# One VectorE running sum in place of seven TensorE sums in three norms, and three late modulation sums moved

## What is computed

```python
mod = silu(c) @ w_mod + b_mod                      # 9 vectors of 1024
sh1, sc1, ga1, sh2, sc2, ga2, sh3, sc3, ga3 = split(mod, 9)
h = modulate(rms_norm(x, g_ffn1), sh1, sc1)
x = x + 0.5 * (1 + ga1) * swiglu(h, w1_gate, w1_up, w1_down)     # first FFN, hidden width 2816
h = modulate(rms_norm(x, g_mix), sh2, sc2)
x = x + (1 + ga2) * hybrid_mixer(h, w_in, ...)                   # 16 attention heads, w_o
h = modulate(rms_norm(x, g_ffn2), sh3, sc3)
x = x + 0.5 * (1 + ga3) * swiglu(h, w2_gate, w2_up, w2_down)     # second FFN
```

## Time and profile before

| | us |
|---|---|
| median of 3 runs | 2854.35 (2852.21 to 2855.42) |
| the profiled execution | 2856.67 |
| its span, first to last instruction | 2854.9 |
| PE busy | 2518.7 (88%) |
| DVE busy | 1047.9 (37%) |
| ACT busy | 465.7 (16%) |
| mean granted TensorE clock | 0.939 of full speed |

### The profile page before, as it was taken

One profiled execution on the slowest core, in us unless ns is written; L12 is line 12 of the kernel. 1 busy time (PEld: TensorE's weight loads), 2 busy tenths in 40 slices (PEclk: granted clock), 3 DMA queues, 4 the chain that ended last, 5 costly groups with the idle time before them and its releaser, 6 DMA issues. The chain is left out here.

```text
span 2854.9 us, 24606 instructions
## 1 busy us (share of the span) xinstructions
PE 2518.7 (88%) x9051; PEld 1170.1 (41%) x9051; DVE 1047.9 (37%) x1236; ACT 465.7 (16%) x732; POOL 179.6 (6%) x458
## 2 busy tenths in 40 slices
PE   8999999999998999999997798688888788878884
PEld 4444444465564444434444454333333233323331
DVE  3655530145462333310106633433333333333334
ACT  2000000155332000000102130011111111111111
POOL 0000000000000000000000000111111111111110
PEclk9999999999899999999998799799899989999997
DMA  7444534122101121413201000799999999999995
GB/s 269 147 147 147 175 129 105 33 51 61 49 1 59 59 88 59 120 41 90 86 19 64 0 8 30 310 413 417 411 412 407 411 406 404 410 405 413 403 413 222
DMA packets 182831, 563.19 MB, mean 197 GB/s; under 512 B 16864, under 2 KB 132848, under 8 KB 156544
## 3 DMA queue, kind: packets, MB, share of 16 engines
q1 hardware_dynamic: 172384, 554.10, 50.8%
q0 software_dynamic: 10400, 8.42, 1.0%
HBM read 567.19 MB, written 20.97 MB: 206 GB/s over the span
## 5 line engine op out<-in xcount | busy, mean ns | idle before, releaser
L1143 PE MATMUL ps<-slot,xT 128*64 128x512 f32 x2048 | 516.4, 663 | 164.6 <-DMA slot<-in_expert_w_up 163.9
L715 PE MATMUL ps<-hT,slot 128*128 128x512 f32 x1408 | 614.4, 597 | 13.0 <-ACT hT L1238 7.2
L715 PEld LDWEIGHTS ps<-hT,slot 128*128 128x128 f32 x1408 | 267.9, 192 | 351.0 <-issue 347.4
L1143 PEld LDWEIGHTS ps<-slot,xT 128*64 128x64 f32 x2048 | 155.6, 152 | 523.5 <-issue 304.5
L743 PE MATMUL ps<-big,slot 128*128 128x512 f32 x704 | 310.4, 601 | 12.0 <-DVE big L1565 6.2
L1974 DVE COPY hT<-ps 128x256 f32<-128x256 f32 x64 | 27.2, 425 | 632.0 <-PE ps L1151 632.0
L1162 PE MATMUL ps<-slot,hT 128*64 128x512 f32 x1024 | 235.6, 602 | 1.2 <-DVE hT L1974 1.2
L1965 DVE RECIPROCAL xT<-xT 64x512 f32<-64x512 f32 x64 | 214.1, 3345 | 2.2
L743 PEld LDWEIGHTS ps<-big,slot 128*128 128x128 f32 x704 | 135.7, 193 | 182.0 <-issue 169.0
L1561 DVE RECIPROCAL eb<-eb 128x512 f32<-128x512 f32 x44 | 147.5, 3353 | 1.5
L1559 DVE TENSOR_SCALAR eb<-eb 128x512 f32<-128x512 f32 x44 | 18.8, 427 | 331.8 <-ACT eb L1248 331.8
(11 more groups left out here) (331 smaller groups left out, 2313.2 us busy)
## 6 DMA issues: line engine op xcount, KB each, us to landing
slot<-in_expert_w_gate SPq DMA_DIRECT2D x64, 2048.0 KB, 19.4
slot<-in_expert_w_up SPq DMA_DIRECT2D x64, 2048.0 KB, 22.7
slot<-in_expert_w_down SPq DMA_DIRECT2D x64, 2048.0 KB, 25.0
slot<-in_w_mod SPq DMA_DIRECT2D x18, 2048.0 KB, 8.0
slot<-in_w_gate SPq DMA_DIRECT2D x22, 1024.0 KB, 5.5
slot<-in_w_up SPq DMA_DIRECT2D x22, 1024.0 KB, 7.9
slot<-in_w_down SPq DMA_DIRECT2D x16, 1408.0 KB, 7.4
slot<-in_w_in SPq DMA_DIRECT2D x24, 512.0 KB, 6.4
```

What stands on the lines that cost most here:

```text
L715: last = mm(ps[:, 2 * j + g, :], w[:, g, k, j * P:(j + 1) * P], hT[:, k, META:TOK], start=(k == 0), stop=(k == KC - 1))
L1143: last = mm(ps[g * CAP:(g + 1) * CAP, j, :], xsT[j][:, k, :], w[g][:, k, :], start=(k == 0), stop=(k == KC - 1))
```

## The change

In norms 1, 2 and 3 TensorE's eight sums become two. ScalarE writes the square of chunk 0 to the first half of `tmp` and all later ones to the second. VectorE adds the squares of chunks 1 to 6 to the first half one after the other (`add_square`, six adds a norm, counted by the new `squares_added`), each ahead of the update of the chunk after. At the end of the stage TensorE sums the first half (chunks 0 to 6) and then the second (chunk 7). Norm 0 is as it was.

In the first FFN, the 12 small matmuls of the last three modulation items move behind norm 1's sums; the third item gets a buffer of its own, `acc_2`. TensorE's wait for `mod_copied` moves there too, and a second one stands ahead of the forget-gate projection (which writes bank 4). VectorE's steps on `modT[:, 60:72]` move behind norm 1. The semaphore `c_exp_ready` is replaced by `scalar_step`.

```diff
-        acc_last = [eb[:, 0, :], eb[:, 1, :], rstd[:, 0:512]]
+        acc_2 = sb("acc_2", [P, 512])
+        acc_last = [eb[:, 0, :], eb[:, 1, :], acc_2[:, :]]
...
-            def norm_sum(r, n):
-                pe.wait_ge(s_sq, KC * r + n + 1)
+            def first_norm_sum(n):
+                pe.wait_ge(s_sq, n + 1)
+                mm(ps[:, 0, :], ones, tmp[:, n % 2, META:TOK], start=(n == 0), stop=(n == KC - 1)).then_inc(s_ss, 1)
+
+            def norm_sum(r):
+                pe.wait_ge(s_add, (KC - 2) * r)
                 for b, (t0, w) in enumerate(HALVES[r]):
-                    last = mm(ps[:, b, 0:w], ones, tmp[:, n % 2, t0:t0 + w], start=(n == 0), stop=(n == KC - 1))
+                    mm(ps[:, b, 0:w], ones, tmp[:, 0, t0:t0 + w], start=True, stop=False)
+                pe.wait_ge(s_sq, KC * (r + 1))
+                for b, (t0, w) in enumerate(HALVES[r]):
+                    last = mm(ps[:, b, 0:w], ones, tmp[:, 1, t0:t0 + w], start=False, stop=True)
                 last.then_inc(s_ss, 1)
...
-                    pe.wait_ge(s_mcp, 1)
                 pe.wait_ge(s_hid, (FC + 2) * r + 2 + FC)
...
-                    if r == 0 and d == 5:
-                        for s in MOD_LAST:
-                            u.take(s, 1)
-                        pe.wait_ge(s_macc, N_GU + len(MOD_LAST))
-                        for n, src in enumerate(acc_last):
-                            mod_sum(src, 4 * n)
-                    if d >= 1:
-
-                        norm_sum(2 * r + 1, d - 1)
-                norm_sum(2 * r + 1, KC - 1)
+                norm_sum(2 * r + 1)
+                if r == 0:
+                    for s in MOD_LAST:
+                        u.take(s, 1)
+                    pe.wait_ge(s_mcp, 1)
+                    pe.wait_ge(s_macc, N_GU + len(MOD_LAST))
+                    for n, src in enumerate(acc_last):
+                        mod_sum(src, 4 * n)
...
             pe.wait_ge(s_late, 48)
+            pe.wait_ge(s_mcp, 2)
...
                 mix(d, j, 0 if d >= 6 else 4, 8).then_inc(s_wo, 1)
-                if j >= 2:
-
-                    norm_sum(2, j - 2)
...
-            norm_sum(2, KC - 2)
-            norm_sum(2, KC - 1)
+            norm_sum(2)
...
-                    if k >= 2:
-                        act.wait_ge(s_ss, KC * r + k - 1)
+                    if r == 0 and k >= 2:
+                        act.wait_ge(s_ss, k - 1)
+                    elif k >= 2:
+                        act.wait_ge(s_add, (KC - 2) * (r - 1) + k - 1)
                     d = MIX_ORDER[k] if r == 2 else k
-                    av(tmp[:, k % 2, t0:t1], xT[:, d, t0:t1], ACT.Square).then_inc(s_sq, 1)
-                act.wait_ge(s_ss, KC * (r + 1))
+                    av(tmp[:, min(k, 1) if r else k % 2, t0:t1], xT[:, d, t0:t1], ACT.Square).then_inc(s_sq, 1)
+                act.wait_ge(s_ss, KC + r)
...
+            def add_square(r, k):
+                t0 = HALVES[r][0][0]
+                dve.wait_ge(s_sq, KC * r + k + 1)
+                v.tensor_tensor(tmp[:, 0, t0:TOK], tmp[:, 0, t0:TOK], tmp[:, 1, t0:TOK], ALU.add).then_inc(s_add, 1)
...
                 for d in range(KC):
-                    if r == 0 and d == KC - 1:
-                        dve.wait_ge(s_msum, N_GU + len(MOD_LAST) + 1)
-                        link(v.tensor_tensor(modT[:, 60:72], ps[:, 4, 0:12], col("b_mod")[:, 60:72], ALU.add))
-                        norm_scale(2)
-                        out_gate(2)
+                    if d >= 2:
+                        add_square(2 * r + 1, d - 1)
                     dve.wait_ge(s_dn, KC * r + d + 1)
...
             norm(1)
+            dve.wait_ge(s_msum, N_GU + len(MOD_LAST) + 1)
+            link(v.tensor_tensor(modT[:, 60:72], ps[:, 4, 0:12], col("b_mod")[:, 60:72], ALU.add))
+            norm_scale(2)
+            out_gate(2)
+            dve.drain().then_inc(s_mcp, 1)
...
             for j, k in enumerate(MIX_ORDER):
+                if j >= 2:
+                    add_square(2, j - 1)
                 dve.wait_ge(s_wo, 6 + j + 1)
```

More of the change, by code:

```diff
@@ L208, in build @@
         s_tro = sem("odd_tiles_turned_copied")
-        s_cexp = sem("c_exp_ready")
         s_cact = sem("c_act_ready")
@@ L217, in build @@
         s_sq = sem("squares_ready")
+        s_add = sem("squares_added")
         s_ss = sem("square_sum_done")
@@ L665, in _ @@
             phase_left(pe, 1)
-            def norm_sum(r, n):
-                pe.wait_ge(s_sq, KC * r + n + 1)
+            def first_norm_sum(n):
[3 more added lines that the diff above has]
+                pe.wait_ge(s_add, (KC - 2) * r)
                 for b, (t0, w) in enumerate(HALVES[r]):
-                    last = mm(ps[:, b, 0:w], ones, tmp[:, n % 2, t0:t0 + w], start=(n == 0), stop=(n == KC - 1))
+                    mm(ps[:, b, 0:w], ones, tmp[:, 0, t0:t0 + w], start=True, stop=False)
+                pe.wait_ge(s_sq, KC * (r + 1))
+                for b, (t0, w) in enumerate(HALVES[r]):
+                    last = mm(ps[:, b, 0:w], ones, tmp[:, 1, t0:t0 + w], start=False, stop=True)
                 last.then_inc(s_ss, 1)
             for n in range(KC):
-                norm_sum(0, n)
+                first_norm_sum(n)
             pe.wait_ge(s_cact, 1)
@@ L1203, in _ @@
             act.wait_ge(s_cols, 16)
-            av(c_exp, col("c"), ACT.Exp, scale=-1.0).then_inc(s_cexp, 1)
+            av(c_exp, col("c"), ACT.Exp, scale=-1.0).then_inc(s_act, 1)
             for t in (1, 3):
@@ L1267, in z_tiles @@
                 return [ps[:, b, at:at + P * (t + 1)] for t, (b, at) in enumerate(Z_AT)]
-            steps = [0]
+            steps = [1]
             def link(ins):
@@ L1505, in _ @@
                               ps[:, 2 * t:2 * t + 2, :].rearrange("p b (k n) -> p (b k) n", k=4)).then_inc(s_trc, 1)
-            dve.wait_ge(s_cexp, 1)
+            dve.wait_ge(s_act, 1)
             link(v.tensor_scalar(c_act, c_exp, 1.0, None, ALU.add))
```

## The result

The changed kernel takes 2837.93 us (median of 6 runs, 2836.46 to 2841.01), the kernel before 2855.37 (6 runs, 2852.21 to 2856.14): 17.4 us less, ratio 0.9943 with an interval of 0.9933 to 0.9953. A second set of 5 runs of the same kernel gave 2836.47 against 2854.79: 18.3 us less, ratio 0.9934 (0.9921 to 0.9946). The forecast was 2834.3, 20.1 us less; the range (2829.5 to 2841.0) holds both medians. Of the 3.6 us between 2837.93 and the forecast, 1.0 is the kernel before, whose median rose from 2854.35 over 3 runs to 2855.37 over 6. The profiled execution took 2837.06 us, its span is 2835.2, 19.7 under the span before.

A forecast was written before the change was run, and what follows sets the result against it. TensorE's stream was taken to bound the three stages with streamed norms, transfers only the last stretch. First FFN 9.99, mixer 4.73 and second FFN 5.34 sum to 20.06 us less: 2834.3 us against the median, range 2829.5 to 2841.

The forecast's parts named there:

- What bounds the three stages: Two FFN down stages and the mixer's output stage: TensorE never pauses, so work removed shortens the stage by its full length.
- The price of a sum: Each sum leaving TensorE's stream saves 0.86 us in the first FFN and mixer, 0.89 in the second FFN.
- Small matmuls and the clock behind them: First FFN, step from chunk 5 to 6: 4.37 us gained, 2.70 small matmuls and 1.67 clock; free at their new place.
- The wait for `mod_copied`: Start of the first FFN's down stage: the first down matmul no longer waits for it and starts 0.46 us earlier.
- The mixer: Mixer's output stage: five sums between updates give 4.30 us and the shorter tail 0.43, together 4.73.
- The adds: VectorE's adds in the three streamed norms cost nothing; bounds were nothing and 0.69 us in each tail.
- The sum: Whole kernel: 9.99 + 4.73 + 5.34 = 20.06 us off, giving 2834.3 us against the median.
- Clock held: Rival, gap ahead of the mixer: small matmuls count as work, mixer starts at full clock, 2831.9 us; chance 0.11.
- Adds in the tail: Rival: an add and a square stand in each of three norm tails, 3.96 us more, 2838.3; chance 0.10.
- Given back to the transfers: Rival, last stretch with the expert loads: the 20 us turn into waiting there, 2854 us, no change; chance 0.05.
- Slower by the attention stretches: Rival: the attention stretches' clock shortfall, 63 us at most, grows; by a half gives 2866 us; chance 0.04.
- The other signs: Signs of being right: no 0.50 clock inside the down stage, FFN steps 19.25 us, first mixer matmul some 10 us earlier.

The follow-up runs named there:

- the run with the wait inside: Changed kernel with TensorE's wait for the bank's update moved from a down chunk's head to ahead of the previous chunk's last matmul: 2834.63 us, ratio 0.9924.
- the modulation alone: Kernel before with only the small matmuls, the wait for `mod_copied` and VectorE's steps moved, eight sums as before: 2849.70 us against 2855.99.
- the norms alone: Changed kernel with the small matmuls, the wait for `mod_copied` and VectorE's steps back at their old places: 2846.68 us, ratio 0.9972.
- the three versions: Changed kernel with unread full-width matmuls in five TensorE gaps: 2829.99 us; bank wait also moved inside the chunk before: 2828.60; then also mixed among small matmuls: 2831.53.

## Why the prediction was right, and what was off

- **What bounds the three stages.** Right. TensorE's stream sets them: every microsecond taken out of it is gone from the stage, and adding 18 operations to VectorE costs nothing (2837.86 against 2837.93 us).
- **The price of a sum.** Mis-sized at ten of seventeen places. In the mixer it is 0.86 us (steps of 4.29 become 3.44 or 3.43). In the FFNs the step from chunk 1 to 2 loses the full 0.86 or 0.89, but the five steps after it come out at 19.38, not at the 19.25 that I had read from chunks 0 to 1. That step has one wait at its head; from chunk 3 on there are two, and a sum ahead of them had hidden the second. The reference step was of another kind than those it was used for. 10 x 0.13 = 1.3 us, shown by the run with the wait inside.
- **Small matmuls and the clock behind them.** Right: 4.37 us, measured alone. At their new place they cost nothing: the mixer starts 5.80 us behind the root, before 5.79. The gap's clock loss is of the old size or a little under: the first 16 records take 8.73 us and 8.77 in the two profiles of the changed kernel and 9.85 with the modulation alone; where nothing filled the gap, 9.48 and 9.91 (the norms alone).
- **The wait for `mod_copied`.** Forecast 0.46, measured 0.50.
- **The mixer.** Forecast 4.73, measured 4.29 + 0.43.
- **The adds.** Forecast nothing, measured nothing, slack 1.29 us as worked out.
- **The sum.** With the 1.3 us taken off, 18.76 were to be expected in the stretches and at the start of the down stage; the profiles show 18.28 + 0.50 = 18.78. The medians show 17.4 and 18.3. What lies between is not in the changed places: the three untouched stretches that repeat differ by -2.6, +1.0 and +3.6 us, 2.0 together, and the expert stretch moves by 3.1 from one execution to the next.
- **Rivals.** Clock held: wrong, shown by the granted clock of 0.50 at the mixer's start and by doubling the small matmuls. Adds in the tail: wrong here, true by estimate from 1.29 us more. Given back to the transfers: not seen, the expert stretch is no longer than before (1039.6 and 1042.7 us, 1043.3 before). Slower by the attention stretches: its sign came, its size did not. In the second block the mean clock fell from 0.88 to 0.86, beyond the 0.01 that the prediction named as a sign of being wrong, and the stretch took 3.6 us more, a sixth of the 21 that would have undone the gain; in the first block's mixer the clock stayed at 0.96 and the stretch was 2.6 us shorter. I gave this rival 0.04 for turning the sign and left its small form out of the forecast's own uncertainty, where it belongs with some 3 us.
- **The other signs.** From 378 us to the end of the down stage the granted clock was 1.00, also where it had stood at 0.50 behind the small matmuls; only at the start of the stage, behind the gap, it read 0.50 (369.7 to 373 us). The steps were 19.38 and not 19.25 us at ten places, and the first mixer matmul came 8.5 us earlier and not 10: the hidden chunks were ready 1.0 us later in this execution, and the waits took 0.65.

Luck had a part in how near the time came: the net of the untouched stretches is small because they moved in both directions.

Not settled: what decides how long the untouched stretches take. A lower mean clock goes along with a longer stretch in every profile without fillers, but no run here moved it on purpose there, and what sets it for a kernel isn't shown.

## What to carry to other kernels

Price a removed step by neighbours that will stand under the same waits afterwards: an instruction in between can be hiding the cost of a wait that was satisfied long ago. The wait for a free buffer cost less here inside the work before it than at the head of the next piece. And where TensorE idles for several microseconds at a known place, full-width matmuls that nobody reads, placed ahead of or between narrow ones and ended before the data is due, gave 5 to 9 us here on top of a change worth 18, 1.3 of them by the moved wait in two of the three versions.

## What the runs showed of the hardware

- Matmuls with a single column keep TensorE busy in the records (3.89 of 4 us) and did not keep its clock. With twelve the clock fell behind them, with twenty-four during them: 2.7 us for the first dozen, 5.3 for the second, at a granted clock of 1.00 and 0.50. With one matmul of 512 columns ahead of every four of them it held through the whole gap (granted clock 1.00 from 524 to 534 us):

```profile
524.00:530.00 6.00, 5.92 (x32) 3.98 (x30) 4.43 (x3) 1.04 (x2) 0.00 (x0) 1.00 0.00 0
530.00:534.00 4.00, 3.40 (x8) 1.63 (x9) 3.97 (x9) 4.00 (x7) 0.00 (x0) 1.00 0.00 0
```

The Trainium skill, "TensorE: Matmul & The Clock Gate", Part 1, says that activity releases the throttle and that the clock follows how busy the array has been. The traces agree with the first (behind the gap of the changed kernel the granted clock is 0.50 from 535 to 538 us and 1.00 from 541 on, under full-width matmuls); for the second, "busy" can't be the busy time of a profile.

- A second satisfied wait at the head of a run of matmuls cost 0.13 us each time, ten times out of ten; inside the run it cost nothing.
- Twice the same kernel: 0.1 us of difference over the 300 us in which TensorE streams, 0.1 over the 408 us of the second block up to the experts, 3.1 over the last 1040, where the transfers are busy (DMA share 0.96).
